# Sparse attention in a two-part transformer kernel: four buffers for transposed maps, and value products issued in pairs

## What is computed

```python
def nsa_mixer(x, w_in, cmp_pos, cmp_w1, cmp_b1, cmp_w2, w_out):
...
        s = jnp.einsum('bgrqd,bgcd->bgrqc', qc, k_cmp, preferred_element_type=f32)
        s = s - sl * (tf[:, None] - cmp_center[None, :])
        p_cmp = masked_softmax(s, m_c) * m_c
        o_cmp = jnp.einsum('bgrqc,bgcd->bgrqd', p_cmp.astype(dt), v_cmp)
...
        o_sel = jnp.einsum('bgrqk,bgqkd->bgrqd', p.astype(dt), vg)
...
        o_win = jnp.einsum('bgrqk,bgkd->bgrqd', p.astype(dt), vw)
        o = (gc[0][..., None] * o_cmp.astype(f32) + gc[1][..., None] * o_sel.astype(f32)
             + gc[2][..., None] * o_win.astype(f32)).astype(dt)
```

## Time and profile before

| | us |
|---|---|
| median of three runs | 3619.75 (3618.88 to 3619.79) |
| the profiled execution, its own time | 3614.65 |
| its span, from first to last instruction | 3612.9 |
| TensorE busy in the span | 3428.7 (95%) |
| VectorE busy | 1702.3 (47%) |
| ScalarE busy | 1149.7 (32%) |
| mean granted TensorE clock | 0.976 of full speed |
| the stage of the change in the span | from 769.4 to 938.0 |

### The profile page before, as it was taken

The page is one execution under the profiler, slowest core; times in us unless marked ns, Lnnn a source line. Parts: engine busy times, 40 slices in busy tenths (PEclk is TensorE's granted clock), DMA queues, the critical chain, the costliest instruction groups (busy, mean ns, idle before and its releaser), DMA issues. The chain is left out here.

```text
span 3612.9 us, 43719 instructions
## 1 busy us (share of the span) xinstructions
PE 3428.7 (95%) x16808; PEld 2368.3 (66%) x16808; DVE 1702.3 (47%) x2890; ACT 1149.7 (32%) x1824; POOL 0.2 (0%) x4
## 2 busy tenths in 40 slices
PE   8899999989999999989998999989988997999997
PEld 6678878866788887746875444437756886444436
DVE  6665544468665537575334111127667334111116
ACT  6632223247522224365322100013356333000003
POOL 0000000000000000000000000000000000000000
PEclk9999999999999999999999999999999998999999
DMA  4222222210122231211225999991221225999992
GB/s 155 85 94 93 98 91 95 94 72 2 71 97 95 93 99 56 77 62 56 95 91 234 407 423 423 423 389 57 85 71 42 94 80 211 380 423 423 423 422 74
DMA packets 113100, 619.20 MB, mean 171 GB/s; under 512 B 12781, under 2 KB 13301, under 8 KB 63545
## 3 DMA queue, kind: packets, MB, share of 16 engines
q1 hardware_dynamic: 112952, 617.17, 44.3%
HBM read 614.94 MB, written 4.28 MB: 171 GB/s over the span
## 5 line engine op out<-in xcount | busy, mean ns | idle before, releaser
L411 PE MATMUL PS<-WK_r,RING_r 128*128 128x512 f32 x1920 | 747.8, 389 | 0.0
L409 PE MATMUL PS<-WK_r 128*128 128x512 f32 x1448 | 565.8, 391 | 0.8 <-DVE RING_r L406 0.8
L411 PEld LDWEIGHTS PS<-WK_r,RING_r 128*128 128x128 f32 x1920 | 359.3, 187 | 77.2
L403 ACT ACTIVATE WK_r<-RING 128x1024 fp32r<-128x1024 f32 x212 | 223.4, 1054 | 448.9 <-PE PS L411 369.8
L410 PE MATMUL PS<-HT_r,WK_r 128*128 128x512 f32 (+1 forms) x896 | 349.2, 390 | 0.0
L406 DVE TENSOR_TENSOR RING_r<-RING,WK_r 128x1024 fp32r<-128x1024 f32 x212 | 259.0, 1222 | 184.9 <-ACT WK_r L403 184.9
L409 PEld LDWEIGHTS PS<-WK_r 128*128 128x128 f32 x1448 | 271.6, 188 | 58.2 <-DVE RING_r L406 1.2
L410 PE MATMUL PS<-HT_r,RING_r 128*128 128x512 f32 (+1 forms) x752 | 294.2, 391 | 0.0
L411 PE MATMUL PS<-AR_r,RING_r 128*128 128x512 f32 x672 | 262.9, 391 | 0.0
L406 DVE TENSOR_TENSOR RING_r<-RING,RING_r 128x1280 fp32r<-128x1280 f32 (+2 forms) x96 | 132.3, 1380 | 275.0 <-ACT RING_r L403 275.0
L409 PE MATMUL PS<-AR_r,RING_r 128*128 128x512 f32 x640 | 251.1, 392 | 9.1 <-DVE HT_r L406 9.1
(11 more groups left out here) (464 smaller groups left out, 5383.5 us busy)
## 6 DMA issues: line engine op xcount, KB each, us to landing
AR<-moe SPq DMA_DIRECT2D x156, 1024.0 KB, 23.2
RING<-moe SPq DMA_DIRECT2D x124, 1024.0 KB, 22.8
EXTRA<-moe SPq DMA_DIRECT2D x78, 1024.0 KB, 21.3
RING<-ff_in SPq DMA_DIRECT2D x96, 512.0 KB, 3.3
RING<-branch SPq DMA_DIRECT2D x64, 640.0 KB, 3.9
WK<-moe SPq DMA_DIRECT2D x26, 1024.0 KB, 25.5
RING<-ff_out SPq DMA_DIRECT2D x48, 512.0 KB, 3.3
RING<-mix_in SPq DMA_DIRECT2D x44, 512.0 KB, 3.3
```

Of the source, the lines that this page charges most:

```text
L403: return nc.scalar.activation(r(out), x, ACT.Copy)
L409: nc.tensor.matmul(out, r(w_high), r(x_high), start=start, stop=False)
L411: return nc.tensor.matmul(out, r(w_low), r(x_high), start=False, stop=stop)
```

## The change

Four buffers take the place of two for the transposed maps, so the copy of item n waits for the value product of item n-4. TensorE issues no value product behind the turning of an odd item, and those of items n-2 and n-1 behind the turning of an even item n. The output of a chunk is copied one item later.

```diff
+        PTN = [wk(6 + 2 * b, 2).rearrange("p (m n) -> p m n", m=2) for b in range(4)]
...
-                                                  PT[n % 2][:, 0, m * P:(m + 1) * P], start=(t == 0), stop=False,
+                                                  PTN[n % 4][:, 0, m * P:(m + 1) * P], start=(t == 0), stop=False,
...
-                                                  PT[n % 2][:, m, kb * P:(kb + 1) * P], start=False,
+                                                  PTN[n % 4][:, m, kb * P:(kb + 1) * P], start=False,
...
                 turn(n)
-                if n:
+                if n and n % 2 == 0:
+                    values(n - 2)
                     values(n - 1)
+            values(ITEMS - 2)
             values(ITEMS - 1)
...
                 act.wait_ge(s["turned"], n + 1)
-                if n >= 2:
-                    act.wait_ge(s["summed_v"], n - 1)
+                if n >= 4:
+                    act.wait_ge(s["summed_v"], n - 3)
                 if compressed:
-                    nc.scalar.activation(PT[n % 2][:, 0, 0:2 * P], bank(6, 0, 2 * P), ACT.Copy).then_inc(s["copied"], 1)
+                    nc.scalar.activation(PTN[n % 4][:, 0, 0:2 * P], bank(6, 0, 2 * P), ACT.Copy).then_inc(s["copied"], 1)
                 else:
                     w = P * (t + 1)
-                    nc.scalar.activation(PT[n % 2][:, :, 0:w], PS[:, 6:8, 0:w], ACT.Copy).then_inc(s["copied"], 1)
+                    nc.scalar.activation(PTN[n % 4][:, :, 0:w], PS[:, 6:8, 0:w], ACT.Copy).then_inc(s["copied"], 1)
...
-                if n >= STEP and n % STEP == 1:
+                if n >= STEP and n % STEP == 2:
                     output(n // STEP - 1)
```

## The result

The changed kernel takes 3631.16 us (median of 8 runs, 3629.27 to 3634.77) against 3620.18 us (median of 8, 3616.96 to 3624.20) before. The ratio is 1.0035, with a 95% interval from 1.0027 to 1.0044: some 12.7 us slower, 9.8 to 15.9 (the medians alone are 11.0 apart). The forecast was 18.5 us slower, 3638.2, with 3634 to 3642 as its own range and 3631 to 3644 as the wide one. The sign was right. The wide range reaches so low because it takes in most of the rival "no gap between paired values", 12.8 us and 3632.5, and that rival is the one that names the size.

What follows compares the result with a forecast made beforehand. The prediction took a ring between TensorE and VectorE as the bound: 4.95 us more per two chunks, 19.8 over four blocks, less about 1.3 at the ends, 18.5 slower, 3638.2 us; own range 3634 to 3642, wide 3631 to 3644.

Steps and rivals of the forecast that it cites:

- no gap between paired values: Rival: the second value group of a pair starts without the 0.16 us gap; 12.8 us slower, 3632.5; chance 0.15.
- What bounds the kernel: Changed stage, 168.60 us: TensorE and VectorE wait for each other (28.9 and 23.3 us), a ring that TensorE nearly fills.
- Buffers, waits, output copy: 0: Freeing buffers sooner, the new buffers' space and the later output copy were each put at 0.
- The ring of a pair of items: Turning, two value groups, score n+3, its masking, weighing n+2, next even turning; nine positions, 45.21 us per two chunks against 40.26.
- The copy path at k=7: Eighth of a chunk's nine items (k from 0): turning n+2 waits for the copy of n+1, 5.29 us.
- How two value groups follow one another: 0.16 taken: Start gap between a pair's value groups on TensorE, kept at 0.16 us because the wait stays; without it 36 pairs lose 5.7.
- TensorE's work in flight "stays near 161": Expected sign: the stage's window grows from 168.6 to about 187 us while TensorE's work in flight stays near 161.
- The ends, 1.3 off 19.8: About 1.0 us back at the stage's start and another 0.3 or so at its end, off the four blocks' 19.8.
- The clock: Rival: TensorE in flight 0.86 of the time, clock falls to 0.89; 31 us slower, 3651; chance 0.05.
- The fastest rival ("PE is the bound"): Rival: VectorE stays ahead, TensorE's work alone sets the time and grouping pays; 10.5 us faster, 3609.3; chance 0.03.

Runs made afterwards that it cites:

- experiment 1: The changed kernel with the value products issued one by one again, in the old order: ratio 0.9994 to the kernel before, stage 170.10 us.
- Experiments 2: The changed kernel with score n+3 issued ahead of the pair of value groups: ratio 0.9990 to the kernel before, stage 166.01 us.
- experiment 4: The changed kernel with score n+3 between the two value groups of an even n: 3620.40 us, ratio 1.0001 to the kernel before, stage 173.48 us.
- experiment 6: The changed kernel with three value groups behind every third turning instead of pairs: 3645.47 us, ratio 1.0074, stage 197.56 us.
- Experiment 3: The kernel before, with 120 already satisfied waits put between the blocks inside value groups: ratio 1.0000, stage 170.18 us.
- Experiment 5: The changed kernel reordered, for even n: turning n, scores n+3 and n+4, turning n+1, values n-1 and n: 3610.92 us against 3619.60 before, ratio 0.9979.

## Why the prediction was right, and where its size was off

*What bounds the kernel.* Right. The two facing waits pointed to a ring between TensorE and VectorE, and the experiments show it: by the order alone they move the stage from 158.68 us to 182.96, with the same matmuls and the same masking (and to 197.56 with groups of three, where the clock has a share).

*Buffers, waits, output copy: 0.* Right for the old order, shown by experiment 1.

*The ring of a pair of items.* Right in form and in all nine positions: the measured steps differ from the forecast's, less one gap, by 0.03 us at most, except k=7 with 0.08. Experiments 2 and 4 take groups out of the ring and experiment 6 puts one in, and the stage follows.

*The copy path at k=7.* Right. The wait appears where it was put, and 5.21 were measured for 5.29. Less the gap it would be 5.13; the 0.08 that are left, the only miss over 0.03, stay open. The banks of the turnings do need a cover that the change takes away, as the Trainium skill's rule in Perfetto Trace Analysis, Matmuls, would have it. The trace agrees, with 2.3 us of such waits in the stage; it is a small share of the 13.2.

*How two value groups follow one another: 0.16 taken.* This is the step that failed, and it is why the forecast was 5.8 us (by the ratio) above the measurement. The term of the sum was 36 times 0.16, 5.7 us; it measured about 0. I reasoned that the gap belongs to the wait, from two scores without a wait between them that had no gap. Those two are also groups of one kind, and the row couldn't tell these apart. Experiment 3 did: waits cost nothing. With the gap out, the ring gives 43.77 per two chunks for 43.78 measured, and 12.8 for the whole against 13.2 in the trace and 12.7 in the runs (11.0 between their medians). The rule that I weighed, from the Trainium skill, TensorE: Matmul & The Clock Gate, The mechanism, that a weight load can be pulled ahead of matmuls in flight, would give this gapless start. The trace agrees: the load of the second value group starts 0.11 ahead of its matmul. Why no load is ahead where the kind changes isn't shown.

*TensorE's work in flight "stays near 161".* It fell to 156.8. The gaps that went, at most 5.7 us, are the likely reason for these 4.3; it wasn't tested. *The ends, 1.3 off 19.8.* The measured period gives 4 times 3.52, 14.1, and the stage is 13.2 longer: 0.9.

*The clock.* In the changed kernel it kept 1.00 outside of the stage's start, with work in flight for 38.18 of 43.78 us, 0.87, so the rival is out. In experiment 6 it fell, with 43.02 of 50.00 us in flight: 0.86, nearly the same share. So the mean share, on which I had weighed the rival, doesn't tell the two cases apart; my 0.05 was right in the outcome, but not for a reason that the traces bear out.

*The fastest rival ("PE is the bound").* It failed because weigh n+2 wasn't done in time: every even turning but one waits for it. Experiment 5 shows what it takes: an order in which the scores stand ahead of the value work.

## What to carry to other kernels

When two in-order engines feed each other, write out the ring: what stands on the first engine between the item that it gets and the item that it must give back. Work that nobody waits for, here the value products, belongs behind the work that closes the ring; grouping it paid only there (experiments 2 and 5). A deeper buffer in itself moved nothing here; see first whether the wait that it removes exists, and then whether it permits a better order.

## What the runs showed of the hardware that I had not expected

On TensorE a start gap of about 0.16 us stands behind a group of turnings or of values when another kind follows, and some 0.2 behind a score (two t=3 scores in a row take 0.22 less than twice one). It is gone between two value groups and between two t=3 scores, though a wait lies between them. Satisfied waits inside a value group don't bring it in. For small groups that is much: a t=0 value group takes 0.37 from start to start, and 0.21 of it is matmuls. And with groups of three the granted clock was 0.50 behind a stretch in which TensorE had work for 2.35 of 4.24 us, with no idle time longer than 1.11 us in it.
